# Rotary turn of the queries moved from TensorE and VectorE into packed rows that pass through DRAM

## The reference

```
x = x + m2 * rmsnorm(rglru_block(h));   x = x + m5 * rmsnorm(conv_ffn(h))      # layer 0
rows, win = shared_kv(x)                   # K/V for three branches; K of two of them is rotated
q = h @ w_qg;  q_rot = rope_partial(q)     # 16 heads of 64; only the first 16 of each head turn
o = g0*compressed(q) + g1*selected(q_rot) + g2*window(q_rot)    # compressed uses q as it is
x = x + m2 * rmsnorm(o @ w_o);          x = x + m5 * rmsnorm(conv_ffn(h))      # layer 1
rope_partial: x1, x2 = q[..., :8], q[..., 8:16];  (x1*cos - x2*sin, x2*cos + x1*sin, q[..., 16:])
```

## Time and profile before

| what | us |
|---|---|
| median of three executions | 3403.19 |
| the profiled execution | 3402.5 |
| its span | 3400.7 |
| stage C's 16 units, about | 1650 to 1772 |
| rotation | 1772.64 to 1806.6 |
| attention and samples, about | 1806.6 to 2402 |

### The profile page before, as it was taken

How to read it: one execution, slowest core, us unless ns; L and a number is a source line. 1 busy time by engine, 2 the same in 40 slices (tenths; PEclk the granted TensorE clock), 3 DMA queues, 4 the chain that set the end, 5 groups by cost and what they waited for, 6 DMA issues and landing times.

```text
span 3400.7 us, 56831 instructions
## 1 busy us (share of the span) xinstructions
PE 3132.8 (92%) x22282; PEld 2840.0 (84%) x22282; DVE 2062.5 (61%) x3765; ACT 816.3 (24%) x1379; POOL 1188.8 (35%) x803
## 2 busy tenths in 40 slices
PE   6997999999999998989777999998889999999995
PEld 4886989999999997989644666675779999999995
DVE  4676186657576576653468888701349585685775
ACT  4554131001010013011125777600131010010011
POOL 1232424434444433333004555400333444444441
PEclk8998999999999998999778999999889999999997
DMA  5222222122222123211253000075221111111112
GB/s 200 79 79 113 83 103 87 63 75 75 75 81 69 44 72 125 88 56 55 92 165 130 2 2 2 4 252 198 94 93 43 44 50 44 44 50 44 50 44 109
DMA packets 76011, 270.43 MB, mean 80 GB/s; under 512 B 8650, under 2 KB 19154, under 8 KB 72546
## 3 DMA queue, kind: packets, MB, share of 16 engines
q1 hardware_dynamic: 73794, 251.53, 21.6%
q10 hardware_dynamic: 1984, 15.62, 1.3%
HBM read 243.29 MB, written 33.10 MB: 81 GB/s over the span
## 4 chain that ended last, share of the span: by engine, by line
PE 70%; issue 15%; DVE 8%; DVEq 2%; ACT 2%; POOL 2%; DMA 1%; POOLq 1%; SPq 0%; ACTq 0%
PE PB L1843 31%; PE PA L1843 31%; DVE ring L1180 2%; POOL ring L1233 1%; PE PA L1879 1%; PE PB L1879 1%; DVE ring L1177 1%; PE PC L281 1%; DMA mt<-in_mw 1%; DMA mw<-in_mw 1%; ACT ring L1149 1%; DVEq L1181 1%; DVEq L2124 0%; PE PC L1954 0%; DVE pt L1188 0%
## 5 line engine op out<-in xcount | busy, mean ns | idle before, releaser
L1627 POOL TENSOR_TENSOR w_hi<-w_raw,misc 128x1024 fp32r<-128x1024 f32 x191 | 370.5, 1940 | 1752.5 <-PE PA L1843 707.5
L1629 POOL TENSOR_TENSOR w_lo<-w_raw,w_hi 128x1024 fp32r<-128x1024 f32 x191 | 561.1, 2937 | 27.2
L1843 PE MATMUL PA<-hB_hi,w_hi 128*128 128x348 f32 x1248 | 268.5, 323 | 0.0
L1843 PE MATMUL PA<-hB_hi,w_lo 128*128 128x348 f32 x1248 | 266.3, 322 | 0.0
L1843 PE MATMUL PA<-hB_lo,w_hi 128*128 128x348 f32 x1248 | 265.7, 321 | 0.0
L1843 PE MATMUL PB<-hB_hi,w_hi 128*128 128x348 f32 x1224 | 262.0, 322 | 0.0
L1843 PE MATMUL PB<-hB_hi,w_lo 128*128 128x348 f32 x1224 | 261.2, 322 | 0.0
L1843 PE MATMUL PB<-hB_lo,w_hi 128*128 128x348 f32 x1224 | 260.8, 321 | 0.0
L1843 PEld LDWEIGHTS PA<-hB_lo,w_hi 128*128 128x128 f32 x1248 | 211.0, 188 | 0.0
L1843 PEld LDWEIGHTS PA<-hB_hi,w_hi 128*128 128x128 f32 x1248 | 210.0, 188 | 0.4
L1843 PEld LDWEIGHTS PA<-hB_hi,w_lo 128*128 128x128 f32 x1248 | 210.1, 188 | 0.0
(11 more groups left out here) (582 smaller groups left out, 7107.8 us busy)
## 6 DMA issues: line engine op xcount, KB each, us to landing
w_raw<-in_w SPq DMA_DIRECT2D x197, 512.0 KB, 3.5
mt<-in_mw SPq DMA_DIRECT2D x48, 1024.0 KB, 5.0
pages<-in_pages SPq DMA_DIRECT2D x64, 384.0 KB, 4.2
x_dram<-X SPq DMA_DIRECT2D x12, 1032.0 KB, 3.9
X<-x_dram SPq DMA_DIRECT2D x3, 4128.0 KB, 13.5
mw<-in_mw SPq DMA_DIRECT2D x4, 2048.0 KB, 22.3
vall<-in_pages_v SPq DMA_DIRECT2D x64, 128.0 KB, 2.5
out_kvT<-kb ACTq DMA_DIRECT2D x12, 516.0 KB, 2.7
```

The lines of the kernel that those rows point to most:

```text
L1627: pool.tensor_tensor(hi, w_raw[b], zero.broadcast_to([P, 1024]), ALU.add)
L1629: pool.tensor_tensor(lo, w_raw[b], hi.bitcast(F32), ALU.subtract).then_inc(sem("w_split"), 1)
L1843: mm = pe.matmul(PS[ps][:, c, 0:width], w[:, w0:w0 + P], x[:, k, c * width:(c + 1) * width], start=(k == 0 and n == 0), stop=(k == K - 1 a ...
```

## The change

1. The rotation after stage C goes. SP copies, before stage C, the 16 turning channels of each head to DRAM (`pack_out`: six DMAs, once in order and once with the halves of 8 swapped), and reads both back as packed rows `qpk` and `qsw`, 128 partitions x 2 x 1032 (`pack_in`), behind `mod_load(32)`, with packed tables. VectorE turns them in three instructions, one each in units 3, 4 and 5. SP writes the result to DRAM and from there into the query tiles (`pack_back`): heads of t = 0 behind `mod_load(43)`, of t = 1 behind `mod_load(47)`. Attention waits for `q_back`.
2. In the K/V stage `aux(10)` moves behind Q's `first_tiles`.
3. In the residuals the first row is added before the second is weighted, and the edge columns follow at once.
4. One extra weight pair instead of two: the fourth tile is split into the ordinary pair, once the second tile is done.
5. The three `prepare` calls of layer 0 move ahead of the last sums of its ConvFFN; the copy of the sample columns (`ts`) moves behind Q's tiles.

```diff
-    WX = [[(view(f"wx_hi{r}{i}", r, [P, 1024], F32R, 16640 + 8192 * i), view(f"wx_lo{r}{i}", r, [P, 1024], F32R, 20736 + 8192 * i))
-           for i in range(2)] for r in range(2)]
+    WX = [(view(f"wx_hi{r}", r, [P, 1024], F32R, 16640), view(f"wx_lo{r}", r, [P, 1024], F32R, 20736)) for r in range(2)]
+    qpk, qsw = view("qpk", 3, [P, 2, TOK]), view("qsw", 3, [P, 2, TOK], F32, 8 * TOK)
+    q_dram = [nc.dram_tensor(f"q_dram{i}", [2 * P, TOK], F32, kind="Internal").ap() for i in range(3)]
@@ ffn_dve
+        if l == 0:
+            prepare(dve, 5)
+            prepare(dve, 13)
+            prepare(dve, 7)
         sums_out(CHUNKS - 1, "last")
@@ kv_pe
-            tile(None, WX[1][n - 2] if n < 4 else n % 2, n % 2, HB, width=CW, freed="hb_free" if n == 11 else None)
+            tile(None, WX[1] if n == 2 else n % 2, n % 2, HB, width=CW, freed="hb_free" if n == 11 else None)
...
-                aux(n - 1)
+                if n < 11:
+                    aux(n - 1)
         first_tiles(T_Q, Q_DONE, 3, Q_EV - 1)
+        aux(10)
         aux(11)
@@ q_dve
+        dve.drain()
+        dve.tensor_copy(ts, QR[:, :, NPR:TOK]).then_inc(sem("ts_kept"), 1)
@@ stage_c_dve
+            if 3 <= u <= 5:
+                rotate_dve(dve, u - 3)
@@ rotate_pe and the old rotate_dve go
+    def rotate_dve(dve, step):
+        tables = [t.unsqueeze(1).broadcast_to([P, 2, TOK]) for t in (cosT, sinT)]
+        if step == 0:
+            dve.wait_ge(sem("qpk_in"), 16 * 4)
+            dve.tensor_tensor(qpk, qpk, tables[0], ALU.mult)
+        elif step == 1:
+            dve.tensor_tensor(qsw, qsw, tables[1], ALU.mult)
+        else:
+            dve.tensor_tensor(qpk, qpk, qsw, ALU.add).then_inc(sem("q_turned"), 1)
+        dve.drain()
+
+    def pack_out(sp):
+        sp.wait_ge(sem("q_scaled"), 8)
+        for h in range(2):
+            sp.dma_start(q_dram[0].rearrange("(n h d) c -> h d n c", h=2, d=16)[h], QR[64 * h:64 * h + 16]).then_inc(sem("qpk_out"), 16)
+            for half in range(2):
+                to = q_dram[1].rearrange("(n h a d) c -> h a d n c", h=2, a=2, d=8)[h][1 - half]
+                sp.dma_start(to, QR[64 * h + 8 * half:64 * h + 8 * half + 8]).then_inc(sem("qpk_out"), 16)
+
+    def pack_in(sp):
+        sp.wait_ge(sem("kb_rotated"), 4)
+        for dst, src in ((cosT, a["cos_packed"]), (sinT, a["sin_packed"])):
+            sp.dma_start(dst, src).then_inc(sem("qpk_in"), 16)
+        sp.wait_ge(sem("kc_done"), 1)
+        sp.wait_ge(sem("qpk_out"), 16 * 6)
+        for i, dst in enumerate((qpk, qsw)):
+            sp.dma_start(dst, q_dram[i].rearrange("(t p) c -> p t c", p=P)).then_inc(sem("qpk_in"), 16)
+
+    def pack_back(sp, t):
+        sp.wait_ge(sem("q_turned"), 1)
+        sp.dma_start(q_dram[2][t * P:(t + 1) * P], qpk[:, t, :]).then_inc(sem("qpk_turned"), 16)
+        sp.wait_ge(sem("qpk_turned"), 16 * (t + 1))
+        sp.wait_ge(sem("sc_done"), 8 * (t + 1))
+        sp.wait_ge(sem("ts_kept"), 1)
+        for h in range(2):
+            sp.dma_start(QR[64 * h:64 * h + 16, 4 * t:4 * t + 4, :],
+                         q_dram[2][t * P:(t + 1) * P].rearrange("(n h d) c -> h d n c", h=2, d=16)[h]).then_inc(sem("q_back"), 16)
@@ att_pe
-        pe.wait_ge(sem("q_rotated"), KT)
+        pe.wait_ge(sem("sc_read"), 16)
+        pe.wait_ge(sem("ct_ready"), 16)
+        pe.wait_ge(sem("oc_done"), 16)
+        pe.wait_ge(sem("md_add"), 18)
+        pe.wait_ge(sem("q_back"), 16 * 4)
@@ SP's program
+        pack_out(sp)
         for p in range(32, 48):
             mod_load(sp, p, mt2)
+            if p == 32:
+                pack_in(sp)
+            if p == 43:
+                pack_back(sp, 0)
+        pack_back(sp, 1)
         smp_sp(sp)
@@ first_splits
-                done = d0 + (-1, 0, 0, 0, 1, 2)[i] if i < 6 else d0 + i - 1
-                split(None, (t0 + i) % 2, 16 * ((t0 + i) // 2 + 1), done, WX[r][i - 2] if i in (2, 3) else None)
+                done = d0 + (-1, 0, 0, 2, 1)[i] if i < 5 else d0 + i - 1
+                split(None, (t0 + i) % 2, 16 * ((t0 + i) // 2 + 1), done, WX[r] if i == 2 else None)
@@ residual
-            for k in range(KT + 1):
...
-                dve.drain()
-                if k == 1 and scale is not None:
-                    dve.tensor_tensor(ts, X[:, :, NPR:TOK], msamp(scale), ALU.mult)
-                    dve.drain()
-                    edge_hi(dve, shift)
+            weighted(0)
+            dve.drain()
+            added(0)
+            if scale is not None:
+                dve.tensor_tensor(ts, X[:, :, NPR:TOK], msamp(scale), ALU.mult)
+                dve.drain()
+                edge_hi(dve, shift)
+            weighted(1)
+            dve.drain()
+            for k in range(2, KT + 1):
+                if k < KT:
+                    weighted(k)
+                added(k - 1)
                 dve.drain()
```

More of the change, by code:

```diff
@@ L209, in build @@
     C["b1c"] = misc[:, 6:8]
-    rx = view("rx", 3, [P, TOK])
+    qpk, qsw = view("qpk", 3, [P, 2, TOK]), view("qsw", 3, [P, 2, TOK], F32, 8 * TOK)
     OC = view("oc", 2, [P, KT, TOK])
@@ L524, in up @@
                     pe.wait_ge(sem("ev_act"), c * 8 + (E0 + 2 * p + b - 1))
-                tile(None, ws[b] if ws else (t0 + b) % 2, (D0 + b) % 2, HB, width=CW)
+                tile(None, ws if ws and b == 0 else (t0 + b) % 2, (D0 + b) % 2, HB, width=CW)
         def down(c, w, last_chunk=False):
@@ L1008, in stage_c_dve @@
         dve.drain()
[L1011 to L1023, removed]
-        dve.drain()
[L1025 to L1028, removed]
-            dve.drain()
-            dve.tensor_tensor(QR[:, n, :], QR[:, n, :], rx, ALU.add).then_inc(sem("q_rotated"), 1)
-            dve.drain()
+    def rotate_dve(dve, step):
[7 more added lines that the diff above has]
+            dve.tensor_tensor(qpk, qpk, qsw, ALU.add).then_inc(sem("q_turned"), 1)
+        dve.drain()
@@ L1459, in smp_sp @@
     def smp_sp(sp):
-        sp.wait_ge(sem("q_rotated"), KT)
+        sp.wait_ge(sem("sel_ready"), 16)
+        sp.wait_ge(sem("oc_done"), 16)
+        sp.wait_ge(sem("q_back"), 16 * 4)
         sp.dma_start(ptab, a["page_table"]).then_inc(sem("ptab_in"), 16)
@@ L2014, in _ @@
         stage_c_pe(pe)
-        rotate_pe(pe)
         att_pe(pe)
@@ L2117, in residual, with weighted, added @@
                 dve.wait_ge(sem("row_out"), n + 1)
-            for k in range(KT + 1):
+            def weighted(k):
+                dve.tensor_tensor(b[f"t{k % 2}_{NREG[n]}"][:, 0:NPR], src[:, k, 0:NPR], rows, ALU.mult)
+            def added(k):
+                dve.scalar_tensor_tensor(X[:, k, 0:NPR], b[f"t{k % 2}_{NREG[n]}"][:, 0:NPR], mcol(gate, k),
+                                         X[:, k, 0:NPR], ALU.mult, ALU.add).then_inc(sem("x_ready"), 1)
+            weighted(0)
[8 more added lines that the diff above has]
+            for k in range(2, KT + 1):
                 if k < KT:
-                    dve.tensor_tensor(b[f"t{k % 2}_{NREG[n]}"][:, 0:NPR], src[:, k, 0:NPR], rows, ALU.mult)
-                if k >= 1:
-                    dve.scalar_tensor_tensor(X[:, k - 1, 0:NPR], b[f"t{(k - 1) % 2}_{NREG[n]}"][:, 0:NPR], mcol(gate, k - 1),
-                                             X[:, k - 1, 0:NPR], ALU.mult, ALU.add).then_inc(sem("x_ready"), 1)
+                    weighted(k)
+                added(k - 1)
                 dve.drain()
-                if k == 1 and scale is not None:
-                    dve.tensor_tensor(ts, X[:, :, NPR:TOK], msamp(scale), ALU.mult)
-                    dve.drain()
-                    edge_hi(dve, shift)
             if scale is not None:
@@ L2260, in _ @@
         ffn_dve(dve, 0)
-        prepare(dve, 5)
-        prepare(dve, 13)
-        prepare(dve, 7)
         residual(1, 3, O0, 5, 13, 12)
@@ L2268, in _ @@
         stage_c_dve(dve)
-        rotate_dve(dve)
         att_dve(dve)
@@ L2329, in _constants @@
     a["perm"], a["cos"], a["sin"] = perm, cos, sin
+    a["cos_packed"], a["sin_packed"] = np.tile(cos[0:16], (8, 1)), np.tile(sin[0:16], (8, 1))
     q = np.arange(P)[:, None, None] + P * np.arange(QT)[None, :, None]
```

## The result

The changed kernel takes 3420.59 us (median of 12 runs, 3408.62 to 3426.77), the kernel before 3403.97 (12 runs, 3401.93 to 3409.61): ratio 1.0039, 95% interval 1.003 to 1.0048. It is 0.4% slower. The forecast was 3406.6, no change, with a range from 3389 to 3420; the time lies 14 us above the forecast and 0.6 above the range, at the price of rival (b), though only a small part of it comes by that rival's mechanism. The profiled execution has a span of 3419.3 us, 18.6 more than before.

A forecast was written before the change was run, and what follows sets the result against it. TensorE's matmuls, busy 3132.8 of 3400.7 us, were taken as the bound, with every added pause paid in full. Saved 47.7, lost 51.1: net 3.4 slower, 3405.9, plus 0.7 for the median gives 3406.6; range 3389 to 3420.

The forecast's parts named there:

- rival (b): Compressed stage: the way through DRAM is too narrow, attention or modulation loads wait; 15 us more, 3421; chance 0.17.
- The large loss: Starts of two ConvFFNs: one extra pair delays split, sixth load and spill; 38.9 us lost, plus 4.2 of low clock.
- Rival (a): ConvFFN starts: the spill isn't late or ScalarE doesn't need it; 43.1 us of loss go, 3363.5; chance 0.07.
- The small gain of the single pair: Residuals and third prepare group: VectorE no longer slowed by GpSimd's fourth-tile split; 8.7 us saved.
- The small orders: Q's first tiles ahead of `aux(10)`, 3.5 us saved, and the new order in the residuals, 1.5 us saved.
- Q's first tiles: Between K/V and Q: moved ahead of `aux(10)`, third tile 6.1 us earlier, less 2.5 for low clock; 3.5 saved.
- The order in the residuals: Residuals: TensorE can begin 1.2 us earlier; 0.5 us saved each, 1.5 in three.
- the price of the rotation's way in the compressed stage: Compressed stage: 4.0 us lost on VectorE's added instructions and 4.0 on SP's added transfers.
- VectorE's steps: Compressed stage: three instructions of 2064 columns, 7.2 us together, partly in VectorE's slack; 4.0 us lost.
- SP and the returns: Compressed stage: stores and returned rows delay modulation loads and attention's start; 4.0 us lost, bounds 0 and 9.
- The 34.0: After stage C: the rotation leaves TensorE's path before the first score; 34.0 us saved if rows are back by then.
- (c): VectorE's steps, Q and the spill: covers are better than taken; 13.3 us better, 3393; chance 0.16.

The follow-up runs named there:

- spill and state first: The changed kernel, single pair kept, with the spill and the conv state's load issued ahead of the sixth weight load: 3369.6 us, ratio 0.9901 to before.
- The pair alone: The kernel before with only the single extra weight pair instead of two: 3441.1 us, ratio 1.0102.
- two pairs: The changed kernel with both extra weight pairs of before put back: 3375.3 us, ratio 0.9913 to before.
- without the way: The changed kernel with spill and conv state ahead of the sixth load, without packed-row transfers and VectorE's turning; attention uses unturned rows: 3360.4 us.
- the fillers alone: The changed kernel with only twenty unread TensorE products of 512 columns added in the compressed stage's pauses: 3404.45 us, ratio 0.9999 to before.
- rotation alone: The kernel before with only the rotation of the packed rows through DRAM: 3388.0 us, ratio 0.9943.
- spill first: The changed kernel, single pair kept, with only the spill issued ahead of the sixth weight load: 3377.6 us, ratio 0.992 to before.

## Why the prediction missed by 14 us

**The large loss was right.** Forecast 38.9 us for the late spill and 4.2 for the clock. The third tile starts 20.0 us after the second one's end in both layers (20.1 forecast). Against the kernel with spill and state first, which keeps the single pair, the stretches before the third tile are longer by 18.3 and 19.6 us, together 37.9. The slow clock shows from the third to the ninth tile: 2.6 and 2.3 more than before, 5.0 together. The pair alone cost 35.6 in its own run; forecast net 34.4 (38.9 + 4.2 - 8.7). Rival (a) is out.

**The small gain of the single pair was right.** 8.7 forecast. The two residuals were summed a little low in the forecast: 1.19 + 1.94 + 2 x 2.40 - 4 x 0.225 is 7.0, not 6.8. From two pairs to spill and state first it is 52.62 - 49.07, 51.58 - 47.76 and 106.51 - 105.55: 8.3 us at the starts of the three stages. In layer 1, however, 4.0 of it are lost again by the ninth tile (141.23 against 137.23), which the forecast didn't see. VectorE's 64-column operations in the changed kernel (answer to the earlier trace rows):

```profile
L2148 DVE TENSOR_TENSOR ts<-ts,modT x4: 225/225/856, 425.7 to 3395.6; 128x64 f32<-128x64 f32 x4
```

```profile
L2150 DVE TENSOR_TENSOR X<-X,ts x4: 226/226/226, 426.6 to 3395.9; 128x64 f32<-128x64 f32 x4
```

**The small orders were about right.** Q's first tiles: 3.5 forecast. The third Q tile comes 4.7 us earlier behind K/V (35.4 against 40.1; 34 forecast), after a pause of 5 us, and TensorE's lower clock takes 1.9 back: 2.8. The order in the residuals shows 0.2 us in layer 0 and 1.2 in layer 1 (52.80 to 52.62, 52.81 to 51.58), and K/V's start takes 0.5 less; 1.5 forecast.

**The step that failed is the price of the rotation's way in the compressed stage, 4.0 for VectorE's steps and 4.0 for SP and the returns.** The returns were priced too low, and the stage's clock had no term. The 34.0 are gone (114.50 without the way, 114.2 worked out). But the stage with the way is 131.88 - 114.2 = 17.7 us longer, not 8. By units against before:

- VectorE's steps: units 3 to 5 take 7.8 + 10.6 + 8.9 against 6.9 + 9.0 + 7.2, 4.2 us. Forecast 4.0. Right in that place, though the run without them shows that the time isn't simply theirs.
- SP and the returns: 5.8 us from unit 10 on, 1.8 more at attention's start (8.8 against 7.1 from the last modulation tile to the first score), 7.6. Forecast 4.0, bounds 0 and 9. The sum took two returns, 516 KB in the units of the profile (528 in its text), at the slope of the spill rows; the step "1.6 us by the slope" failed, since those rows are of 128 partitions. At the 115 GB/s above 516 KB take 4.6 us, an estimate. Moving the returns to the end won 1.9 to 4.6 us.
- The clock, units 6 to 9: 34.1 us against 27.4, 6.7 us. Forecast 0, for no term of the sum stood there. The text said of the stage that "the modulation loads hang on TensorE's progress, nothing catches it up", and took the clock into account only after the pauses in front of Q's third tile and at the ConvFFNs' starts.
- The first three units are 0.9 shorter.

That leaves the size. The profiled spans differ by 18.6 us where 3.4 were forecast. Of the 15.2 between, 9.7 are in this stage: 6.7 of clock and 3.6 of returns, less what the first units gave. Another 3.2 lie ahead of all that the change touches and 2.7 in attention, both within the scatter of the profiles; that part of the miss is chance.

How much the clock costs in the median isn't shown by one profile. Nine of the 12 runs take 3416 us or more, with mean clocks of 0.944 to 0.948, and three 3408 to 3412, with 0.948 to 0.951, which fits a long slow stretch in most of the runs but wasn't looked at in more than one. With the fillers alone all 11 lie between 3402.6 and 3408.05, at 0.956 to 0.959. So the clock of the compressed stage can be worth 16 us, more than the whole miss. This doesn't make the 14 us all clock: the fillers also remove slow clock that before has (0.53 from 1742 to 1773), and the returns' 3.6 us are still in. That the filled kernel comes out at the forecast's time is in part luck.

**Of the rivals,** (b) gave the right time, 3421, by luck, with half of its mechanism: the returns are too narrow, but TensorE waits 2.42 us for the last one, not 8, and 4.84 in the middle. It would have given 3421 from the transfers alone; they bring 3.6 of its 15. (c) did not come.

**What stays open:** what decides whether an execution gets the long slow stretch. From modulation tile 32 to the first score five profiled kernels with the same code there took 131.9 (changed), 133.3 (two pairs), 129.5 (rotation alone), 124.3 (spill first) and 124.4 (spill and state first). The new work isn't needed for it: in the kernel before with the single pair alone, which has none of it in this stage, units 7 to 9 took 8.3, 9.0 and 8.3 us against 6.4, 6.6 and 6.3 in before. The stage without any of the new work still has a clock of 0.74. So the 6.7 us are shown to be clock, but not that the way through DRAM brought it on. That the steps of VectorE could be left out with no gain fits a stage whose length the clock sets, but was not tried with fillers.

## What to carry to other kernels

When a buffer is taken away, follow the wait that moves through every queue behind it: here one split held one load, and that held a spill that two engines needed, for 43 us; reordering two lines of the queue kept most of the saving and removed the loss. The stage here, with short pauses of TensorE in every unit, ran at two speeds, 6.6 or 8.3 us for unit 7 with the same code, so that a few microseconds won on another engine didn't show; look at the granted clock of such a stage, not at the mean, and try filling the pauses before trimming the other engines. Price a transfer by a row with the same number of partitions, not by its bytes.

## What the runs showed that was not expected

- Twenty useless products made a kernel 16 us faster (3420.6 to 3404.45), and its spread shrank from 18 us to 5.5.
- The clock stayed at 1.2 GHz for 58 us on end (the stretch 1698.4 to 1756.4 has a granted clock of 0.50) with TensorE busy 87% in units 6 to 9.
- Rows of 16 partitions come back slowly: 1032 KB in 12.65 us and at 115 GB/s, with the DMA engines 99% busy, against 4128 KB in 13.5 us to 128 partitions and 3.9 us for 1032 KB from them.
- The four spill pieces, issued back to back, land 11.4 us after the last issue; spread over the residual each landed in 3.9. Hidden under the first tiles they cost nothing.
